# The first pick of expert rows made one head at a time, with the second pick's sorts moved into the gathering stage

## What is computed

```python
def block(xb):                                   # 128 tokens
    q = (xb @ w_pq).reshape(PEER_BLOCK, PEER_HEADS, 2, D_KEY // 2)
    s1 = jnp.einsum('thk,nk->thn', q[:, :, 0], sub_keys1)
    s2 = jnp.einsum('thk,nk->thn', q[:, :, 1], sub_keys2)
    v1, i1 = lax.top_k(s1, PEER_TOPK)            # 16 of 128
    v2, i2 = lax.top_k(s2, PEER_TOPK)
    cand = (v1[..., :, None] + v2[..., None, :]).reshape(...)
    sc, ci = lax.top_k(cand, PEER_TOPK)          # 16 of 256
    e = i1[ci // 16] * N_KEYS + i2[ci % 16]
    g = jax.nn.softmax(sc, axis=-1)
    a = jax.nn.gelu(jnp.einsum('td,thkd->thk', xb, peer_u[e]))
    return jnp.einsum('thk,thkd->td', g * a, peer_v[e])
```

## Time and profile before

| | us |
|---|---|
| three runs | 1953.71, 1959.49, 1967.63 |
| median | 1959.49 |
| span of the profiled execution | 1949.2 |
| own time of the profiled execution | not shown apart from the runs |
| PE / DVE / ACT / POOL busy in the span | 1459.8 / 1346.5 / 794.0 / 785.3 |

### The profile page before, as it was taken

The page is one execution under the profiler, slowest core; times in us unless marked ns, Lnnn a source line. Parts: engine busy times, 40 slices in busy tenths (PEclk is TensorE's granted clock), DMA queues, the critical chain, the costliest instruction groups (busy, mean ns, idle before and its releaser), DMA issues.

```text
span 1949.2 us, 23852 instructions
## 1 busy us (share of the span) xinstructions
PE 1459.8 (75%) x7204; PEld 694.2 (36%) x7204; DVE 1346.5 (69%) x3201; ACT 794.0 (41%) x2756; POOL 785.3 (40%) x796
## 2 busy tenths in 40 slices
PE   7999987775786877767856766666866666688986
PEld 6765573332232343324322222222321333222331
DVE  6967998865748878888877744444445467885665
ACT  2132247872424444444543443333333223354544
POOL 0953324342343444544433333333333344454442
PEclk9999998997897899889987888888878787898989
DMA  7012689999999999999999999999999999999997
GB/s 299 1 44 92 198 332 409 405 389 421 391 390 399 407 403 421 419 421 421 412 406 420 395 412 420 421 421 420 422 412 423 422 422 410 420 381 418 413 409 296
DMA packets 101025, 723.17 MB, mean 371 GB/s; under 512 B 12017, under 2 KB 12785, under 8 KB 20785
## 3 DMA queue, kind: packets, MB, share of 16 engines
q0 software_dynamic: 82944, 604.02, 75.7%
q1 hardware_dynamic: 17968, 117.77, 15.3%
HBM read 714.78 MB, written 4.87 MB: 369 GB/s over the span
## 4 chain that ended last, share of the span: by engine, by line
DMA 34%; PE 23%; DVE 14%; ACT 7%; issue 6%; POOL 1%; POOLq 0%; ACTq 0%; DVEq 0%
DMA R<-d_uv,W 34%; PE bank L1394 12%; DVE R L2148 8%; PE bank L1155 3%; PE bank L1288 2%; ACT W L1668 1%; ACT L1665 1%; POOL R L912 1%; PE bank L1147 1%; PE bank L1201 1%; ACT W L1673 1%; PE bank L1314 1%; PE bank L1284 1%; PE bank L995 1%; ACT W L1636 1%
## 5 line engine op out<-in xcount | busy, mean ns | idle before, releaser
L912 POOL DMA_INDIRECT R<-d_uv,W x576 | 679.1, 1179 | 1003.6 <-PE bank L1394 764.9
L1394 PE MATMUL bank<-R,W 128*32 128x512 f32 x2296 | 704.5, 719 | 443.6 <-ACT W L1673 423.8
L2148 DVE CUSTOM_DVE_ANT_0 R<-R,W 128x1024 f32<-128x1024 f32 x576 | 696.1, 1223 | 450.7 <-DMA R<-d_uv,W 443.1
L1394 PEld LDWEIGHTS bank<-R,W 128*32 128x32 f32 x2296 | 194.8, 122 | 827.4 <-ACT W L1673 568.7
L1636 ACT CAST W<-W 128x2 uint32<-128x2 f32 x292 | 55.7, 192 | 874.7 <-DVE W L2148 869.5
L1673 ACT ACTIVATE W<-W 128x32 f32<-128x32 f32 x576 | 153.5, 313 | 9.4
L1668 ACT ACTIVATE W<-W 128x1 f32<-128x1 f32 x576 | 138.2, 287 | 9.5
L1314 PEld LDWEIGHTS bank<-E 128*128 128x128 f32 x864 | 101.8, 196 | 27.0 <-issue 26.6
L956 PE MATMUL bank<-E,W 128*128 128x256 f32 (+1 forms) x384 | 102.3, 425 | 10.1 <-DMA E<-d_xT 8.0
L1314 PE MATMUL bank<-E 128*128 128x128 f32 (+1 forms) x864 | 107.4, 281 | 0.1
L956 PEld LDWEIGHTS bank<-E,W 128*128 128x128 f32 x384 | 75.0, 199 | 31.4 <-issue 10.2
(11 more groups left out here) (324 smaller groups left out, 1737.5 us busy)
## 6 DMA issues: line engine op xcount, KB each, us to landing
E<-d_kc SPq DMA_DIRECT2D x8, 2560.0 KB
E<-d_w_pq SPq DMA_DIRECT2D x6, 2048.0 KB, 12.2
E<-d_vc SPq DMA_DIRECT2D x8, 1536.0 KB, 25.8
R<-d_uv,W POOLq DMA_INDIRECT x576
E<-d_w_out SPq DMA_DIRECT2D x4, 2048.0 KB, 12.1
E<-d_vc SPq DMA_DIRECT2D x8, 1024.0 KB, 30.1
W<-d_w_in SPq DMA_DIRECT2D x3, 2048.0 KB, 21.3
W<-d_w_pq SPq DMA_DIRECT2D x3, 2048.0 KB, 8.1
```

The source lines that it names most:

```text
L912: pool.indirect_dma_start(ring[r], None, A["uv"], bass.IndirectOffsetOnAxis(ap=stage[:, half, s:s + 1], axis=0),).then_inc(landed[r], 16)
L1394: last = mm(acc[TG * js[s]:TG * js[s] + TG, half * 512:half * 512 + 512], wsel[:, r, :], ring[r][:, D + half * 512:D + half * 512 + 512], ...
L2148: last = nc.vector.tensor_tensor_reduce(ring[r][:, 0:D], ring[r][:, 0:D], hrep[:, js[s], :], 1.0, 0.0, ALU.mult, ALU.add, dots[:, x, s:s + 1])
```

## The change

Pick (0,0) is made in two pieces. Head 0 has its own copy of the query (two quarters of four), match, sorts, cross, resolve (`resolve_head`) and lay (`lay_of_head`: its 16 columns), and the first gathers use it alone. Head 1 follows behind `first_stage`. The four sorts of pick (0,1) move from the front to pairs 1 and 2 of the stage, its cross, resolve and lay from pairs 0 to 5 to pairs 3 to 8, and `product_rest(1)` from the front to pair 6. The query (0,1) moves behind `glu_block 3`, and `gelu 3` and the exponential of head 0 ahead of `gate_block 2`. `free(5, 0)` moves ahead of the first sorts. On DVE `lay_too(0)` waits for the last gate.

```diff
         if n == 15:
-            order += [("ask_out", 0, 0), ("match", 0, 0), ("match_out", 0, 0), ("skip_term", 14), ("product_rest", 1)]
+            order += [("ask_out", 0, 0), ("match", 0, 0), ("match_out", 0, 0), ("skip_term", 14)]
         if n == steps:
-            order += [("ssm_out", 15), ("tops", 0, 0, 0), ("skip_term", 15)]
+            order += [("ssm_out", 15), ("free", 5, 0), ("tops", 0, 0, 0), ("tops", 0, 0, 1), ("skip_term", 15), ("gelu", 3)]
...
-            order += [("turn", 0), ("turn_out", 0), ("gate_block", 1), ("ssm_out", 14), ("ask", 0, 0, 0), ("ask", 0, 0, 1)]
-    order += [("glu_block", 2), ("gate_block", 2), ("gelu", 3), ("ask", 0, 1, 0), ("glu_block", 3), ("gate_block", 3), ("ask", 0, 1, 1), ("ask_out", 0, 1)]
-    order += [("tops", 0, 0, 1), ("tops", 0, 0, 2), ("tops", 0, 0, 3), ("match", 0, 1), ("match_out", 0, 1)]
-    order += [(what, 0, 0, x) for what in ("cross", "resolve") for x in range(2)]
-    order += [("lay", 0, 0, 0), ("lay_too", 0, 0, 1), ("first_stage",), ("alpha",)]
-    order += [("tops", 0, 1, j) for j in range(4)]
-    order += [("free", 5, 0), ("ask", 0, 2, 0), ("ask", 0, 2, 1), ("free", 1, 2), ("ask_out", 0, 2)]
+            order += [("turn", 0), ("turn_out", 0), ("gate_block", 1), ("ask", 0, 0, 0), ("ask_out_head",), ("ssm_out", 14),
+                      ("match_head",), ("match_out_head",), ("ask", 0, 0, 1)]
+    order += [("glu_block", 2), ("cross", 0, 0, 0), ("resolve_head", 0), ("gate_block", 2), ("glu_block", 3), ("gate_block", 3)]
+    order += [("lay_head", 0), ("lay_too", 0), ("first_stage",), ("ask", 0, 1, 0), ("ask", 0, 1, 1), ("ask_out", 0, 1)]
+    order += [("tops", 0, 0, 2), ("tops", 0, 0, 3), ("cross", 0, 0, 1), ("resolve_head", 1), ("lay_head", 1), ("lay_too", 1)]
+    order += [("alpha",), ("match", 0, 1), ("match_out", 0, 1)]
+    order += [("ask", 0, 2, 0), ("ask", 0, 2, 1), ("free", 1, 2), ("ask_out", 0, 2)]
...
     for b in range(1, QB):
-        if b > 1:
-            at[GLU_AT + 3 * (b - 1)].append(("product_rest", b))
+        at[GLU_AT + 3 * (b - 1) - (1 if b == 1 else 0)].append(("product_rest", b))
...
         for j in range(4):
-            if n > 1:
-                at[when[j]].append(("tops", b, c, j))
+            at[when[j]].append(("tops", b, c, j))
...
-    pick(1, 0, 0, 0, 0, 0, 1, 2, 3, 4, 5)
+    pick(1, 1, 1, 2, 2, 3, 4, 5, 6, 7, 8)
...
             def experts(p0, p1):
 
                 last = (p1 + 2 * HALF // PAIR) * PAIR - 1
+                if p0 == 0:
+                    act.wait_ge(laid_too, 2)
...
             def first_stage():
                 act.wait_ge(in_fold, 16)
-                act.wait_ge(laid, 1)
+                act.wait_ge(head_laid, 1)
                 act.wait_ge(laid_too, 1)
...
+            def lay_too(e):
+                if e == 0:
+                    dve.wait_ge(sig_ready, QB)
+                    dve.wait_ge(head_picked, 1)
+                else:
+                    dve.wait_ge(picked, 1)
+                lay_of_head(nc.vector.tensor_copy, e, 1).then_inc(laid_too, 1)
```

More of the change, by code:

```diff
@@ L587, in build @@
         gx_ready, gexp_done, picked, laid = (sem(n) for n in ("gx_ready", "gexp_done", "picked", "laid"))
+        head_asked, head_copied, head_matched, head_shown = (
+            sem(n) for n in ("head_asked", "head_copied", "head_matched", "head_shown"))
+        head_gx, head_exp, head_picked, head_laid = (
+            sem(n) for n in ("head_gx", "head_exp", "head_picked", "head_laid"))
         spread_full, hrep_ready = sem("spread_full"), sem("hrep_ready")
@@ L667, in lay_half, with lay_of_head @@
                                     eg[TG * j:TG * j + TG, :, 8 * s + g0 - 8 * c:8 * s + g0 - 8 * c + first])
+            return last
+        def lay_of_head(copy, e, x):
+            for j in range(2 * x, 2 * x + 2):
+                for s in range(SG):
+                    to = egall[TG * s:TG * s + TG]
+                    of = eg[TG * j:TG * j + TG, :, PK * e + SG * s:PK * e + SG * s + SG]
+                    if e == 0:
+                        c0 = HALF * (j // 2) + j % 2
+                        copy(to[:, :, c0:c0 + 3:2], of[:, :, 0:2])
+                        last = copy(to[:, :, 2 * SG + j:3 * SG + j + 1:SG], of[:, :, 2:4])
+                    else:
+                        last = copy(to[:, :, 4 * SG + j:7 * SG + j + 1:SG], of)
             return last
@@ L1315, in ask, with match_head @@
                                   hT[:, k, 0:m], start=(k == 0), stop=(k == DC - 1))
+                if n == 0 and x == 0:
+                    last.then_inc(head_asked, 1)
                 if x == asked(b) - 1:
                     last.then_inc(pq_full, 1)
+            def match_head():
+                pe.wait_ge(in_keys, 16)
+                pe.wait_ge(head_copied, 1)
+                for j in range(2):
+                    last = mm(bank[:, 3, j * P:j * P + P], qpT[:, 0, j * P:j * P + P], keysT[:, j, :], start=True, stop=True)
+                last.then_inc(head_matched, 1)
             def match(b, c):
@@ L1327, in match @@
                     pe.wait_ge(s_ready, n - 1)
-                for j in range(4):
+                for j in range(2 if n == 0 else 0, 4):
                     last = mm(bank[0:m, (3, 1)[c % 2], j * P:j * P + P],
@@ L1405, in _ @@
                      "free": free, "project_first": project_first, "project": project, "spread": spread_h,
-                     "turn": turn, "ask": ask, "match": match, "experts": experts, "gate_turn": gate_turn,
+                     "turn": turn, "ask": ask, "match": match, "match_head": match_head,
+                     "experts": experts, "gate_turn": gate_turn,
                      "gate": gate, "s_scores": s_scores, "s_scores_rest": s_scores_rest, "s_turn": s_turn,
@@ L1632, in resolve, with resolve_head, lay_head @@
                     f(gx[0:m], gx[0:m], ACT.Exp).then_inc(gexp_done, 1)
+            def resolve_head(e):
+                act.wait_ge(gx_ready if e else head_gx, 1)
+                f(gx[:, e, :], gx[:, e, :], ACT.Exp).then_inc(gexp_done if e else head_exp, 1)
+            def lay_head(e):
+                act.wait_ge(picked if e else head_picked, 1)
+                lay_of_head(nc.scalar.copy, e, 0).then_inc(laid if e else head_laid, 1)
             def copy_stage(half, x, at):
@@ L1641, in lay @@
                 last = lay_half(nc.scalar.copy, b, c, x)
-                if x == 1 or 4 * b + c == 0:
+                if x == 1:
                     last.then_inc(laid, 1)
@@ L1700, in _ @@
                      "turn_out": turn_out, "ask_out": ask_out, "match_out": match_out, "resolve": resolve,
-                     "lay": lay, "experts": experts, "gate_turn_out": gate_turn_out, "gate_sigmoid": gate_sigmoid,
+                     "lay": lay, "ask_out_head": ask_out_head, "match_out_head": match_out_head,
+                     "resolve_head": resolve_head, "lay_head": lay_head, "experts": experts, "gate_turn_out": gate_turn_out, "gate_sigmoid": gate_sigmoid,
                      "finish_root": finish_root,
@@ L2015, in tops @@
                 n = 4 * b + c
-                if j == 0:
+                if n == 0 and j == 0:
+                    dve.wait_ge(head_shown, 1)
+                elif j == (2 if n == 0 else 0):
                     dve.wait_ge(s_ready, n + 1)
```

49 lines of the change are left out of this document (38 added, 11 removed).

## The result

| | before | after |
|---|---|---|
| median of the runs of this comparison, us | 1960.24 (1953.71 to 1967.63) | 1975.8 (1967.55 to 2086.21) |
| span of the profiled execution, us | 1949.2 | 1965.5 |
| mean granted TensorE clock | 0.883 | 0.874 |

The ratio is 1.0082, 95% interval 1.0055 to 1.0108: some 16 us slower, where I had forecast no change (1960, range 1951 to 1967). The one run at 2086 was disturbed and doesn't count in the ratio. The direction is that of rival D, whose time was 1964. The 10.3 us that I put around the span in the sum are a misreading: every execution with both numbers on record lasts 1.8 to 2.1 us longer than its span, so the profile of before is of a short execution (some 1951 us), and the other 8.5 us are the distance from it to the median. As a forecast of the median the 1960 stands.

What follows compares the result with a forecast made beforehand. DMA engines were taken as the bound from the first gather on. Head start -7.4, load +5.0, empty queue +2.3 and second ramp +0.8 gave +0.7 us: span 1949.9, with 10.3 around it 1960 us, range 1951 to 1967.

Steps and rivals of the forecast that it cites:

- rival D: DVE, 285 to 315 us: second pick's sorts delay dots and slots, the queue drains; 3.7 us on 0.7, 1964; chance 0.18.
- The 10.3 us that I put around the span: Whole kernel: median of 1959.49 us less profiled span of 1949.2, added to the forecast span of 1949.9 to give 1960.
- The ring covers that: Stage, pairs 6 and 7: queued gathers cover DVE being up to 3.7 us later.
- I take 0, with 3.7 as the other end: Stage: end-time cost taken for 9.1 us more DVE work; 0 us, or 3.7 at the other end.
- from the first gather on the DMA engines set the pace: Gathers onward: the end moves only by bytes or lost DMA time; a gather is 1.05 MB, 2.5 us.
- The idle 0.76 us before a dot: DVE before the dot at 307.09 us: idle 0.76 us for a gather, read as dots waiting for landings.
- the 5.9 us of queued gathers: Ahead of gather 13, 297.05 to 307.09 us: other gathers in front of it, taken as cover for DVE's lag.
- The head start: Start of the gathers: gather 0 at 259.2 us, 7.4 us earlier.
- Query 3: PE, block 0: ends 3.2 us later, at 279.3 instead of 276.05; gathers 6 and 7 start at 280.2 and 281.4.
- the stall of 0.94 us: PE idle ahead of the last matmuls of query 3; if it doesn't come again, the stream's bound is -0.2 us.
- The load of w_pq: Part 0 for block 1, issued at 261.7 us among the gathers: its 2.1 MB cost 5.0 us, bounds 0 and 6.0.
- The empty queue ahead of gather 8: Gather 8 issued at 287.4 us, flowing from 289.0: DMA engines have nothing for 2.3 us, then a ramp of 0.8.

Runs made afterwards that it cites:

- e5: Kernel before with the second pick's sorts and pick and block 1's product moved into the stage, plus two zero-weight matmuls ahead of pairs 1 to 26; ratio 0.9992.
- e6: Kernel before plus only the filler: two zero-weight TensorE matmuls of 512 columns ahead of each of pairs 1 to 26; ratio to before 0.9959.
- e2: Kernel before with only the stage part: second pick's sorts and pick and block 1's product moved into the stage, first pick whole; ratio to before 1.0056.
- e3: Changed kernel with gate 2 ahead of head 0's exponential and half of query (0,1) between glu_block 2 and 3; ratio to before 1.0068.
- e4: Kernel before with the load of w_pq part 0 for block 1 released by the third query instead of the second; ratio to before 1.0034.
- e9: The whole change plus the filler of two 512-column zero-weight matmuls ahead of each of pairs 1 to 26; ratio to before 1.0006.
- e10: Changed kernel with the second pick's sorts back in the front, plus the zero-weight filler ahead of pairs 1 to 26; ratio to before 1.0007.
- e7: e1 with block 1's product and one block 0 sort ahead of the first lay, and the gate 2 order of e3; ratio to before 1.0057.
- e8: e2 with block 1's product back in the front, so only the second pick's sorts and pick move into the stage; ratio to before 1.0055.
- e1: Changed kernel with the second pick's four sorts back ahead of the stage and its cross, resolve and lay at pairs 0 to 5; ratio to before 1.0018.

## Why the prediction was wrong

**The step that failed** is the one on the stage: "The ring covers that" and "I take 0, with 3.7 as the other end." The load costs 9.3 us at a nearly full clock (e5 against e6) and 13.9 at the clock that this kernel gets; by the ratio of e2, 11 us (6 to 16). The error lies one step further up, in "from the first gather on the DMA engines set the pace". The row that I drew it from covers 700 to 1000 us. The idle 0.76 us before a dot was no exception (six dots up to 317 waited so), but a short wait for a landing shows slack of its own size on DVE and not who sets the pace: behind 282 us the chain of waits of before goes through DVE, ACT and PE. The engines' loop is as long as the DMA pace and has nothing to catch up with, so what is added stays. The second term that I didn't have at all is the lower granted clock: 4.6 us in the count by the stage load (13.9 less 9.3), 6.5 by the change (14.2 less 7.7).

**Rival D** had the right engine and queue, and the wrong size: 3.7 on top of 0.7 against 16. It was to decide "once the lag passes the 5.9 us of queued gathers". From 295 to 320 us the share stands at 1.00 and then falls to 0.68, which looks like a queue that runs out late. Whether 5.9 us is the limit is not shown, since no run sets a lag just under it; what is shown is that of a load of 9.1 us nothing, or nearly nothing, is covered.

**The head start** was forecast at -7.4 us for gather 0 and measured at -3.7 (262.88 for 259.2). Two things ate the rest. glu_block 2 starts 2.6 us later, since PE waits 1.10 us for ACT's copy of the turned h, a wait that ssm_out 14 filled before, and runs on at the lower clock behind it; I had 0.8. (In e3, whose program is the same up to there, the clock didn't fall behind the same wait and it is 1.5: that part is chance.) And glu_block 3 came at 252.62 (forecast 250.4) and took 1.7 us longer at the lower clock. e3 took the second away and moved the end by nothing that can be told.

**Query 3** ended at 282.3 (forecast 279.3), gather 6 at 283.2 (280.2), gather 8 at 290.6 (287.4): each 3 us late. glu_block 3 ended 4.0 us later than forecast (258.1 for 254.1), and the stall of 0.94 us ahead of the last matmuls of query 3 didn't come again, as the bounds had allowed. The chain of reasoning was right and its start was off.

**The load of w_pq** was right for the kernel before: forecast 5.0 us, measured 3.5 to 5.0 in gathers and 6.7 (1.4 to 12) in the ratio of e4. In the change the stage load hides it.

**The empty queue ahead of gather 8** is in the profile of after (share 0.94 and 0.81 from 283 to 295), as forecast.

Of the 16 us, then: with the filler 7.7 to 9 us remain (e9 against e6), which is the size of the DVE work moved into the loop. 15 us go away when the filler is added to the change, 8 of which it also takes from the kernel before. So about 7 us of the change's loss are clock that the change loses in addition; by the intervals of the three ratios this is 7, give or take 8, and it rests on the 6.5 us of the gather count and on its second step. What the head split costs by itself at the full clock is open: e10, which should have priced it, didn't hold the clock.

## What to carry to other kernels

Find what bounds each stage by the chain of waits in that stage, and read it before the DMA share: a share of 1.00 and a loop of engines of the same length look alike there, and the work moved into this one was paid in full or nearly so. Where matmuls are short and stand behind waits, compare the duration of equal groups of matmuls; if it has two values and PE is on the chain, work that is thrown away can be worth more than work that is saved. That holds only where PE is on the chain: over the whole kernel the same filler lost 1.1%.

## What the runs showed of the hardware

The granted clock has the two levels 1.2 and 2.4 GHz (the same eight matmul records take 3.83 or 1.92 us), and in this kernel it falls where PE has waited, though not each time: in after a pair takes 3.83 us behind waits of 4.75 and 3.39 us, 2.12 behind one of 0.37, and behind one of 1.92 it takes 2.12 in one place and 3.78 in another. The Trainium skill describes it in "TensorE: Matmul & The Clock Gate", section HAM oscillation: matmuls that wait for data fall back to the lower clock again and again. The rows agree, with the waits here being for ScalarE and not for data. What I hadn't expected is its size in a kernel bound by transfers for most of its span (8 us of 1960 in the kernel before by the ratio of e6, 4.2 in its gather count), and how it may hide small gains: e7 and e8 each took 2.3 us of work out of the stage, came out at a clock 0.08 and 0.07 lower than e1 and e2, and gained nothing. That the clock is the reason in these two is argued and not shown: over all their executions the mean clock of the whole span hardly differs (medians 0.874 in e7 and 0.875 in e1, 0.869 in e8 and 0.872 in e2).
